# The order of the weight loads in a two-block transformer: the small projection stands third in each group of the gate's loads, the compression's loads take every third place

## The reference

```python
# first block (h is 256 x 2048)
z = rms_norm(h) @ w_in                         # 4656 columns
u, g_lru, q, kc, vc, ksel, vsel, kw, vw, gts = split(z)
y_lru = rglru_mixer(u, g_lru, ...)             # convolution and gated recurrence
y_nsa = nsa_mixer(q, kc, vc, ..., gts, ...)    # attention: compressed + selected + window
h = h + rms_norm(concat(rms_norm(y_lru), rms_norm(y_nsa)) @ w_out)
f = square(relu(rms_norm(h) @ mlp_w1)) @ mlp_w2
h = h + rms_norm(f)
h = h + sigmoid(h @ ple_gate) * (p @ ple_proj) # ple_gate 2048 x 2048, ple_proj 256 x 2048

# inside nsa_mixer, for keys and for values:
blk = windows(t) + pe                          # 15 windows of 32 tokens, per key-value group
kc = gelu(blk @ w1) @ w2                       # w1 is 2048 x 256: "the compression"

# second block: a context of 256 tokens and the tokens x pass through w_in_2
# (2048 x 6656, for the context "in2_0c", for x "in2_0"), attention, pooling,
# convolution and w_out_2, twice
```

## Time and profile before

| what | us |
|---|---|
| median of three runs (lowest, highest) | 3212.2 (3209.96, 3218.76) |
| the profiled execution's own time | 3217.07 |
| its span | 3215.4 |
| TensorE busy | 2860.1, 89% |
| VectorE, ScalarE, GpSimd busy | 1653.0, 1138.0, 164.0 |

### The profile page before, as it was taken

The page is one execution under the profiler, slowest core; times in us unless marked ns, Lnnn a source line. Parts: engine busy times, 40 slices in busy tenths (PEclk is TensorE's granted clock), DMA queues, the critical chain, the costliest instruction groups (busy, mean ns, idle before and its releaser), DMA issues. The chain is left out here.

```text
span 3215.4 us, 32172 instructions
## 1 busy us (share of the span) xinstructions
PE 2860.1 (89%) x13308; PEld 2243.1 (70%) x13308; DVE 1653.0 (51%) x1877; ACT 1138.0 (35%) x1389; POOL 164.0 (5%) x172
## 2 busy tenths in 40 slices
PE   5999899999999999999778998786599799996668
PEld 3777788888888888888556887432388678784356
DVE  3644556655545445454335444797533522346954
ACT  3452244444433333334223332353311411232433
POOL 0000100000000000011001000010000200000000
PEclk9998899999999999999888999899799899997779
DMA  6877464466656565655234666799232233464033
GB/s 227 278 248 238 139 232 148 151 237 195 206 185 195 184 196 183 196 183 188 71 144 166 211 221 222 296 348 362 101 137 92 99 124 119 155 217 171 1 135 131
DMA packets 284892, 589.27 MB, mean 183 GB/s; under 512 B 13522, under 2 KB 21562, under 8 KB 282192
## 3 DMA queue, kind: packets, MB, share of 16 engines
q1 hardware_dynamic: 261088, 512.13, 47.6%
q0 software_dynamic: 11552, 48.25, 4.0%
q10 hardware_dynamic: 12112, 26.91, 2.3%
HBM read 560.41 MB, written 26.84 MB: 183 GB/s over the span
## 5 line engine op out<-in xcount | busy, mean ns | idle before, releaser
L1599 DVE TENSOR_TENSOR wlo<-raw,whi 128x2048 fp32r<-128x2048 f32 x304 | 689.0, 2267 | 900.1 <-ACT whi L1112 899.8
L1112 ACT ACTIVATE whi<-raw 128x2048 fp32r<-128x2048 f32 x304 | 575.9, 1894 | 1139.3 <-PE ps L657 907.4
L655 PE MATMUL ps<-whi,ax_hi 128*128 128x512 f32 (+1 forms) x1376 | 540.4, 393 | 0.2 <-DVE wlo L1599 0.2
L657 PE MATMUL ps<-whi,ax_lo 128*128 128x512 f32 (+1 forms) x1376 | 535.0, 389 | 0.0
L656 PE MATMUL ps<-wlo,ax_hi 128*128 128x512 f32 (+1 forms) x1376 | 534.7, 389 | 0.0
L655 PE MATMUL ps<-whi,ay_hi 128*128 128x512 f32 x1056 | 423.2, 401 | 43.7 <-DVE wlo L1599 43.7
L656 PE MATMUL ps<-wlo,ay_hi 128*128 128x512 f32 x1056 | 417.0, 395 | 0.0
L657 PE MATMUL ps<-whi,ay_lo 128*128 128x512 f32 x1056 | 416.9, 395 | 0.0
L1592 DVE TENSOR_TENSOR wlo<-raw,whi 128x2048 fp32r<-128x2048 f32 x84 | 192.3, 2292 | 384.8 <-ACT whi L1104 384.4
L1104 ACT ACTIVATE whi<-raw 128x2048 fp32r<-128x2048 f32 x84 | 160.5, 1914 | 455.7 <-PE ps L616 450.3
L655 PEld LDWEIGHTS ps<-whi,ax_hi 128*128 128x128 f32 x1376 | 262.0, 190 | 76.5 <-issue 21.3
(11 more groups left out here) (366 smaller groups left out, 2805.1 us busy)
## 6 DMA issues: line engine op xcount, KB each, us to landing
raw<-in_w_in_dram SPq DMA_DIRECT2D x192, 1024.0 KB, 5.1
raw<-in_mlp_w_dram SPq DMA_DIRECT2D x128, 1024.0 KB, 5.3
raw<-in_w_mod_dram SPq DMA_DIRECT2D x96, 1024.0 KB, 8.4
raw<-in_w_out_dram SPq DMA_DIRECT2D x48, 1024.0 KB, 5.1
raw<-in_ple_gate_dram SPq DMA_DIRECT2D x16, 1024.0 KB, 5.6
z<-zst POOLq DMA_DIRECT2D x22, 512.0 KB, 4.4
z<-zsc POOLq DMA_DIRECT2D x13, 512.0 KB, 3.4
h<-in_x_dram POOLq DMA_DIRECT2D x2, 2048.0 KB, 10.9
```

Source lines behind the costliest of these rows:

```text
L655: mm(dst, hi_[:, kk, tt], whi[:, x.s % 2, k, 0:w], start=(kk == 0), stop=False)
L657: ins = mm(dst, lo_[:, kk, tt], whi[:, x.s % 2, k, 0:w], start=False, stop=(kk == KT - 1))
L1112: A(whi[:, x.s % 2, :, 0:w], raw[:, x.slot, :, 0:w], ACT.Copy).then_inc(hi_ready, 1)
L1599: V.tensor_tensor(wlo[:, x.s % 2, :, 0:w], raw[:, x.slot, :, 0:w], f32v(whi[:, x.s % 2, :, 0:w]), ALU.subtract).then_inc(lo_ready, 1)
```

## The change

The list of loads gets another order in two places, and the programs of TensorE, ScalarE and VectorE follow it. In the gate's stage the order becomes: unit (i,0), unit (i,1), pp i, unit (i,2), unit (i,3), for all four chunks. TensorE multiplies pp 0 behind unit (0,2) as before, but pp 1, pp 2 and pp 3 behind unit (i,0). In the context's product, the compression's four loads stand behind context units 4, 6, 8 and 10 instead of 3, 4, 5 and 6, and their matmuls run behind units 4, 6, 8 and 10 instead of 4 to 7. Everything of the attention that follows in the three generators is due three slots later.

```diff
-        order += ["in2_0c"] * 4 + ["cmp", "in2_0c"] * 4 + ["in2_0c"] * 40
+        order += ["in2_0c"] * 5 + ["cmp", "in2_0c", "in2_0c"] * 4 + ["in2_0c"] * 35
         order += ["out1"] * 16 + ["in2_0c"] * 4 + ["mlp"] * 128
-        order += (["pp"] + ["gate"] * 4) * 4 + ["in2_0"] * 52
+        order += ["gate", "gate", "pp", "gate", "gate"] * 4 + ["in2_0"] * 52
...
                 for x in CMP:
-                    yield 4 + x.u
+                    yield 4 + 2 * x.u
...
-                yield 8
+                yield 11
...
-                    yield 9 + n
+                    yield 12 + n
...
-                yield 9 + len(BATCH) + 6
+                yield 12 + len(BATCH) + 6
                 prep("nsa")
...
                 hand_unit(x, AY_)
-                if x.u == 2:
+                if x.u == (0 if x.i else 2):
                     y = PP[x.i]
...
# ScalarE
-                yield 7
+                yield 10
                 act.wait_ge(plain_used, BY["cmp"].p0 + 4)
...
-                    yield 9 + n
+                    yield 12 + n
...
-                yield 9 + len(BATCH) + 3
+                yield 12 + len(BATCH) + 3
...
# VectorE
-                yield 8
+                yield 11
                 dve.wait_ge(ev("cmp_o"), 1)
...
-                    yield 9 + n
+                    yield 12 + n
...
-                yield 9 + len(BATCH) + 4
+                yield 12 + len(BATCH) + 4
                 norm("nsa")
```

## The result

The changed kernel takes 3158.40 us (median of four runs, 3153.48 to 3158.95); the kernel before took 3215.48 beside it (3209.96 to 3219.36). The ratio is 0.982, its 95% interval 0.980 to 0.9841: 57 us less, with an interval of 51 to 64. The forecast was 3157, the sum of the terms 55.3 us.

A forecast was written before the change was run, and what follows sets the result against it. TensorE, busy 89% of the span, was taken as the bound, losing time where late ring slots stalled it. Gate 49.5 plus compression 5.8 gave 55.3 us off the 3212.2 median: 3157, own range 3150 to 3164, 8 in 10 within 3148 to 3171.

The forecast's parts named there:

- The gate: Gate's stage: reordered loads remove four TensorE stalls and the low clock after them, 49.5 us less.
- g11: Gate unit (1,1)'s load, still tied to pp 0: split done 4 us before it is needed, so no stall.
- The clock's term: Gate's stage: lower clock after the stalls costs 11.2 us, which goes with them; units then take 5.44 us each.
- The compression: Context product beside the compression: stalls of 3.49 and 0.29 us and 2.0 us of low clock go, 5.8 us less.
- the bound of 6.5: Compression: upper bound of its gain in us, counting the matmul drains of a few tenths ahead of each stall.
- unit 7: Context unit taking the first compression load's slot: ready by 396.5, needed at 398.4, two microseconds of slack against the worst landing.
- The total: Whole kernel: 55.3 us less, median forecast 3157 us, all of it arriving at the end.
- The rival of the bias tables: Late bias tables G, up to 15.4 us landing against 15.1, cancel the compression's gain: 3163 us; chance 8%.
- the gate's first hand-over: Rival: unit (1,1)'s load lands late and TensorE still stalls, up to 12.2 us back, 3157 to 3169; chance 7%.
- the order did what it says: Against the rival that the order changes nothing: something else held SyncE, four gate stalls stay, 3212 us; chance 2%.
- Slower: Rival: late projection loads pp 1 to 3 block TensorE, over 0.3% (9.6 us) slower, needing 65 us of waits; chance 1%.
- TensorE's busy time: Sign in the changed profile, whole kernel: busy time falls by some 13 us, its share rises to about 90%.

The follow-up runs named there:

- e3: Changed kernel with only the new list of loads; the small projection's matmuls stay behind unit (i,2) in all four groups; 3160.29 us, ratio 0.9831 to the kernel before.
- e5: Changed kernel with the gate's old list of loads (projection first in each group), matmuls in their new place; 3168.22 us, ratio 0.9863 to the kernel before.
- e6: Changed kernel with the projection's load second in each group and its matmuls behind unit (i,2) in all groups; 3180.73 us, ratio 0.9903 to the kernel before.
- e2: Kernel before with the compression's part of the change alone, the gate's part left out; 3207.24 us, ratio 0.9982 to the kernel before.
- e7: Changed kernel with VectorE's additions for the compression's windows cut in two, the values' half moved to slot 5; 3157.11 us, ratio 0.9827 to the kernel before.
- e4: Changed kernel run again without any edit, as yardstick; 3159.49 us, ratio 0.9832 to the kernel before.
- e8: Changed kernel run a third time without any edit, as yardstick for its group; 3163.21 us, ratio 0.9844 to the kernel before.

## Why the prediction was right

**The gate: right, 49.67 for 49.5.** The cause, a slot handed over in the last moment, is shown by e3, e5 and e6 from three sides. The two terms are shown as well: the stalls of the earlier trace rows, 37.8, and the clock the rest, 11.9. The slack of g11 was worked out at 4 us and is 4.0, and pp 1 made no wait.

**The clock's term: right in size.** The stretch is at 1.00 and a unit takes 5.44 us, as in the earlier trace rows. By an estimate from the 215.7 ns of the Trainium skill (TensorE: Matmul & The Clock Gate, "Wait — 56ns, not 53.3ns?") the 84.67 us would have been some 3.4 shorter; the trace doesn't agree, 21.77 / 96 = 227 ns.

**The compression: right, 6.03 for 5.8.** e2 shows it alone. The difference is within the bound of 6.5 that counted the overlap ahead of each stall. The prediction feared most for unit 7, with 2 us of slack against the worst landing. Its split waited for TensorE to free the buffer and not for its load:

```profile
385.20 1.92 ACT L1112 ACTIVATE whi<-raw 128x2048 fp32r<-128x2048 f32 x1 [7.15 <-PE ps L657]
```

The low half was ready at 387.15 + 2.29 = 389.44, and TensorE came to the unit at 393.87: 4.4 us of slack.

**The total: partly luck.** The forecast of 3157 stands 1.4 us from the first median, 3158.40, and three timings of the same kernel gave 50 to 57 us less, against 55.3 forecast. The two stretches have 55.7. The prediction said that all of it should arrive at the end; the last stretch is 1.95 us longer in the profile, which it had at nothing, and the first is 4.45 shorter by chance. The totals can't confirm the sum to a microsecond: the three medians of this one kernel lie 4.8 us apart. The terms are confirmed by their stretches.

**The rival of the bias tables: a larger slack than I gave it.** I had 15.4 us of landing against 15.1 of cover. The two loads of G went out at 423.1 and 423.6 and landed, in us from issue to landing (minimum, median, maximum),

```profile
L1275 ACTq DMA_DIRECT2D G<-bias_d x2: 464/494/525, 423.1 to 423.6; - x2
...
DMA to landing us min/median/max: 8.3/11.0/13.7
```

and VectorE read G first at

```profile
439.92 0.31 DVE L1856 SCALAR_TENSOR_TENSOR sc<-ps,G 128x30 f32<-128x30 f32 x2
```

16.8 us behind the first issue. The later load had landed by 423.6 + 13.7 = 437.3 at the latest, so 2.6 us of slack at least. The cover was 1.7 us longer than my 15.1, by the two small groups of matmuls that I named but did not add, and the slowest landing 1.7 shorter than in the earlier trace rows. The prediction could not separate G's own pace from the burst. Two later loads of the same line and size help: issued one at a time, at 479.5 and 528.6 us, they landed in (us, again minimum, median, maximum)

```profile
DMA to landing us min/median/max: 4.2/4.6/5.0
```

So most of the 8.3 to 13.7 us goes with the burst, in which SyncE issued three units' loads at 423.09.

**The other rivals.** No stall at the gate's first hand-over, no wait for pp 1 to 3, and the order did what it says. "Slower" was far off: even with one unit less of cover (e6) the gate's stretch keeps 142.04 - 114.54 = 27.5 of its 49.7 us, and the whole kernel is 31 us below the kernel before (ratio 0.9903), the compression's 6 among them.

**What I gave as one edit was two.** The prediction priced the list and the move of the matmuls together. e3 and e5 show that the list does all, and that the move alone would have done three quarters (142.04 - 105.08 = 37.0 of 49.7).

**TensorE's busy time** fell by 17.4 us (2860.1 to 2842.7), not 13. The gate's stretch has 11.8 of it and the compression's 2.3, together 14.1; 3.8 lie ahead of L758, which the change doesn't touch, and the last stretch is 0.4 higher. In two more profiles of the changed kernel the sum is 2840.8 and 2849.6.

## What to carry to other kernels

In a ring of buffers, count for every load the work that the consumer still has between its last use of the slot and its need of what comes into it, and compare it with the whole chain (issue, landing, conversion). A small transfer that is used late, ahead of large ones, holds its slot longest; put it where the load that follows in its slot is needed two units later, here 10.9 us against 9.4. That was enough by 0.5 us only (e3); using the small transfer earlier as well made it 4.0. A stall of TensorE costs more than its own length: in this kernel 2 to 3 us of lower clock each, so short stalls cost more than their sum in the table of waits.

## What the runs showed that I had not expected

The price in clock grows much less than the length of the stall. Behind 2.04 us it was 1.9 (e7 against the changed kernel), behind 4.0 us 1.9, 1.9 and 3.1 (e6), behind 9.4 to 9.6 us 2.9 to 3.1 (12.42 each in the kernel before, 12.7 in e5). So the shortest of these stalls nearly doubles.

The start of a run is not as steady as its middle. The same work up to context unit 0 took 340.6 to 345.6 us in three profiles of the changed kernel. The granted clock from 300 to 320 us differed, 0.90 in the fastest (e4) and 0.77 in the slowest (e8) of the three:

```profile
300.00:320.00 20.00, 17.03 (x137) 13.39 (x136) 6.15 (x12) 5.80 (x7) 0.00 (x0) 0.90 0.90 302
```

```profile
300.00:320.00 20.00, 20.00 (x126) 15.10 (x124) 4.57 (x9) 3.49 (x5) 0.00 (x0) 0.77 0.75 236
```

What sets when the clock falls there was not tried and stays open. The spread of 5.0 us is nearly as large as the compression's whole gain, which is why that part was read from a stretch and not from the total.
